# Three layer norms of a two-block transformer: the scaling by the inverse deviation moved from VectorE into the product that turns the tile

## The chip, the cores and the metric

The kernel runs on one core of one Trainium2 chip. The metric is the device time of one execution in microseconds (us). TensorE (PE) has two clocks, 1.2 and 2.4 GHz; the profile gives the granted clock as a share of 2.4 GHz. PEld is TensorE's loading of the stationary operand, DVE is VectorE, ACT is ScalarE, POOL is GpSimd, SP is the engine that issues the weight transfers. ACTq and SPq are the queues through which ACT and SP issue transfers.

## The reference

256 tokens of width 1024 pass through two blocks of two layers each. The change touches the layer norms of the first block alone: the one on the input, the one behind the first mixer and the one behind the feed-forward. Cut to what matters:

```
def layer_norm(x, g, b):
    mu = jnp.mean(xf, axis=-1, keepdims=True)
    xc = xf - mu
    var = jnp.mean(xc * xc, axis=-1, keepdims=True)
    y = xc * lax.rsqrt(var + LN_EPS) * g + b

h = layer_norm(x, ln_in_g, ln_in_b)
for layer in range(DEPTH):                       # DEPTH = 2
    proj = h @ w_in[layer]
    ...
    mix = jnp.concatenate([y_pool, y_sb], axis=-1) @ w_out[layer]
    h = layer_norm(DN_ALPHA * h + mix, ln1_g[layer], ln1_b[layer])
    f = swiglu(h, ...) if layer % 2 == 0 else moe_ffn(h, ...)
    h = layer_norm(DN_ALPHA * h + f, ln2_g[layer], ln2_b[layer])
```

## The kernel before

The 256 tokens are two tiles, t = 0 and 1, of 128 partitions (`TT` = 2). `k.h` holds them with tokens on the partitions. The products need the transpose, features on the partitions, and they are made in float32 from two reduced-precision parts: `k.x[0]` is the high part and `k.x[1]` the rest (low part); a weight is split in the same way into `w_high` (cast by ACT, L358) and `w_low` (DVE, L369). Weights stream from memory in loads of 1 MB, two pieces each, in five raw buffers; `PAIRS` = 4 pieces can stand split ahead of TensorE. A cast of piece n waits until TensorE has used piece n - 4 (`k.used`), and TensorE waits for a piece's low part (`low_made`).

Every engine has its own program, in order; the order is written out by hand and semaphores join the engines. Where a layer norm stands between two runs of products, this happens for each tile:

- DVE adds the residual (`vector_residual`, L628, two instructions), takes the moments (`vector_moments`, L580 to L588), subtracts the mean and multiplies by the gain (`vector_centre`, L594), multiplies by the inverse deviation and adds the shift (`vector_scale`, L604). It signals `normed`.
- ACT makes the inverse deviation in four small steps from the reciprocal of the variance (`scalar_layer_norm`, L614 to L620): a root, a half square, a Newton factor `step`, and `rstd = step * root`, which signals `root`.
- TensorE turns the tile in eight transposes of 128x128 into two banks (`tensor_transposes`, L498), each group of four signalling `turned`. While it waits for a tile it multiplies constants into a bank that nobody reads (`tensor_spin`, L485).
- ACT copies each turned bank to `k.x[0]` (L510, `x_high_made`), DVE subtracts this from the bank for `k.x[1]` (L521, `x_made`).
- The first product (`first_product`, L416 and L422) starts with the high part and takes the low part at the end of each piece.

Tile 1's residual must wait for the last of the product before; tile 0's can start earlier, since `tensor_tail` finishes tile 0 first. A float32 product that is not a transpose shows as two MATMUL instructions in the trace; a transpose shows as one.

The gain and the shift are sent to all 128 partitions of `k.gains` by a transfer of 512 KB each (`scalar_gains`, L662 and L663). For the first norm SP issues them behind the input and ahead of the weights (`sync_first`, L2522).

The site at the start is called the start; the one behind the first mixer, whose turned tiles go into the feed-forward, the feed-forward site; the one behind the feed-forward, ahead of the second mixer, the second mixer's site.

## Time and profile before

| | before |
|---|---|
| time, median of 3 runs (range) | 2132.32 us (2129.55 to 2132.45) |
| span of the profiled execution, first to last instruction | 2127.0 us |
| TensorE busy | 2102.8 us, 99% of the span |
| VectorE busy | 1537.3 us, 72% |
| ScalarE busy | 1349.5 us, 63% |
| mean granted TensorE clock | 0.997 of 2.4 GHz |

The span of the profiled execution is its own time between its first and its last instruction; the 5.3 us by which the median is above it lie outside of these or between executions. Busy shares are means over the whole program. What a change at one place is worth must be read from the waits at that place.

### The profile page before, as it was taken

Reading aid. Unit: us, or ns where it says so; the run is one execution under the profiler, and the core shown is the slowest. Engines: PE = TensorE matmul, PEld = TensorE weight load, DVE = VectorE, ACT = ScalarE, POOL = GpSimd, SP = SyncE. Lnnn points to the kernel's source line nnn. Section 1 sums busy time; section 2 is a strip of 40 time slices with the busy share of each in tenths; the row PEclk is TensorE's granted clock in tenths of the full one; section 3 lists DMA queues with packets and bytes.
Section 4 is the critical chain, followed back from the end, with each engine's and each line's share of the span. In section 5 each row is a group of like instructions: output and inputs, shape, how many; then the busy total and the mean of one; then the engine's idle time right before and its main releaser. Section 6 shows DMA issues by size and latency. Waiting matters only on the chain.

```text
span 2127.0 us, 31761 instructions
## 1 busy us (share of the span) xinstructions
PE 2102.8 (99%) x13318; PEld 1889.9 (89%) x13318; DVE 1537.3 (72%) x1701; ACT 1349.5 (63%) x1610; POOL 48.1 (2%) x45
## 2 busy tenths in 40 slices
PE   9999999999999999999999899999999999999998
PEld 8899989888888888888888799998998999998987
DVE  5565565699999899989999777566654686666544
ACT  5554446688878877887878574574553754755543
POOL 0000000100000000000000000000210000000200
PEclk9999999999999999999999999999999999999999
DMA  9366554499999999999999555634655565545652
GB/s 303 119 206 194 197 183 139 146 362 358 341 358 370 332 375 351 367 337 365 358 364 371 195 185 165 197 126 154 208 199 197 178 190 163 175 147 164 199 198 79
DMA packets 301733, 511.43 MB, mean 240 GB/s; under 512 B 10512, under 2 KB 177552, under 8 KB 301584
## 3 DMA queue, kind: packets, MB, share of 16 engines
q1 hardware_dynamic: 296896, 499.68, 68.8%
q10 hardware_dynamic: 4688, 9.65, 1.4%
q8 instruction: 107, 1.75, 0.3%
q14 instruction: 42, 0.34, 0.0%
HBM read 503.53 MB, written 1.05 MB: 237 GB/s over the span
## 4 chain that ended last, share of the span: by engine, by line
PE 96%; DVE 2%; ACT 1%; issue 0%; DMA 0%; ACTq 0%; DVEq 0%
PE bank L389 28%; PE bank L391 28%; PE bank L390 28%; PE bank L485 2%; PE bank L1851 1%; PE bank L416 1%; PE bank L1428 1%; PE bank L1307 1%; PE bank L1365 1%; PE bank L498 1%; PE bank L422 1%; PE bank L2114 1%; DVE w_low L369 1%; PE bank L2090 0%; PE bank L2099 0%
## 5 line engine op out<-in xcount | busy, mean ns | idle before, releaser
L369 DVE TENSOR_TENSOR w_low<-raw,w_high 128x1024 fp32r<-128x1024 f32 x938 | 1135.9, 1223 | 413.0 <-ACT w_high L358 398.1
L358 ACT CAST w_high<-raw 128x1024 fp32r<-128x1024 f32 x938 | 979.7, 1052 | 454.3 <-PE bank L391 434.9
L389 PE MATMUL bank<-x,w_high 128*128 128x256 f32 x1712 | 478.5, 279 | 0.0
L390 PE MATMUL bank<-x,w_high 128*128 128x256 f32 x1712 | 474.9, 277 | 0.0
L391 PE MATMUL bank<-x,w_low 128*128 128x256 f32 x1712 | 474.9, 277 | 0.0
L389 PE MATMUL bank<-w_high,x 128*128 128x512 f32 (+1 forms) x976 | 342.2, 351 | 0.0
L391 PE MATMUL bank<-w_high,x 128*128 128x512 f32 (+1 forms) x976 | 337.8, 346 | 0.0
L390 PE MATMUL bank<-w_low,x 128*128 128x512 f32 (+1 forms) x976 | 337.8, 346 | 0.0
L389 PEld LDWEIGHTS bank<-x,w_high 128*128 128x128 f32 x1712 | 322.2, 188 | 0.4
L390 PEld LDWEIGHTS bank<-x,w_high 128*128 128x128 f32 x1712 | 322.4, 188 | 0.2
L391 PEld LDWEIGHTS bank<-x,w_low 128*128 128x128 f32 x1712 | 321.7, 188 | 0.0
L391 PEld LDWEIGHTS bank<-w_high,x 128*128 128x128 f32 x976 | 183.2, 188 | 23.5
L389 PEld LDWEIGHTS bank<-w_high,x 128*128 128x128 f32 x976 | 183.4, 188 | 23.1 <-DVE w_low L369 0.6
L390 PEld LDWEIGHTS bank<-w_low,x 128*128 128x128 f32 x976 | 183.4, 188 | 22.1 <-issue 0.5
L389 PE MATMUL bank<-w_high,moe_hidT_high 128*128 128x512 f32 x352 | 138.6, 394 | 0.0
L391 PE MATMUL bank<-w_high,moe_hidT_low 128*128 128x512 f32 x352 | 137.3, 390 | 0.0
L390 PE MATMUL bank<-w_low,moe_hidT_high 128*128 128x512 f32 x352 | 137.1, 389 | 0.0
L389 PE MATMUL bank<-w_high,mlp_hid_high 128*128 128x512 f32 x256 | 99.8, 390 | 0.0
L390 PE MATMUL bank<-w_low,mlp_hid_high 128*128 128x512 f32 x256 | 99.7, 389 | 0.0
L391 PE MATMUL bank<-w_high,mlp_hid_low 128*128 128x512 f32 x256 | 99.6, 389 | 0.0
L391 PEld LDWEIGHTS bank<-w_high,moe_hidT_low 128*128 128x128 f32 x352 | 66.1, 188 | 14.0
L390 PEld LDWEIGHTS bank<-w_low,moe_hidT_high 128*128 128x128 f32 x352 | 66.2, 188 | 13.2
(343 smaller groups left out, 2557.3 us busy)
## 6 DMA issues: line engine op xcount, KB each, us to landing
raw<-in_moe_wd SPq DMA_DIRECT2D x88, 1024.0 KB, 5.8
raw<-in_w_in SPq DMA_DIRECT2D x84, 1024.0 KB, 5.3
raw<-in_moe_wg SPq DMA_DIRECT2D x80, 1024.0 KB, 6.0
raw<-in_moe_wu SPq DMA_DIRECT2D x80, 1024.0 KB, 6.0
raw<-in_w_up SPq DMA_DIRECT2D x32, 1024.0 KB, 5.5
raw<-in_w_down SPq DMA_DIRECT2D x32, 1024.0 KB, 4.9
raw<-in_w_out SPq DMA_DIRECT2D x16, 1024.0 KB, 4.9
raw<-in_ffn_wg SPq DMA_DIRECT2D x11, 1024.0 KB, 5.3
```

Of the source, the lines that this page charges most:

```text
L358: q.copy(high, raw).then_inc(st.cast, 1)
L369: q.tensor_tensor(low, raw, high.bitcast(F32), ALU.subtract).then_inc(st.low_made, 1)
L389: T.matmul(out, stationary[0], moving[0], start=start, stop=False, skip_group_check=True)
L390: T.matmul(out, stationary[0], moving[1], start=False, stop=False, skip_group_check=True)
L391: return T.matmul(out, stationary[1], moving[0], start=False, stop=stop, skip_group_check=True)
L416: T.matmul(out[:, j, :], w[:, kk, j * P:(j + 1) * P], k.x[0][:, i, :], start=(i == 0 and j == 0 and w is piece[0]), stop=False, skip_group ...
L422: mm = T.matmul(out[:, j, :], piece[0][:, kk, j * P:(j + 1) * P], k.x[1][:, i, :], start=False, stop=(i == KT - 1), skip_group_check=True)
L485: k.nc.tensor.matmul(k.banks[bank][:, 0:2 * P], k.shared[:, 0:P], k.shared[:, 0:2 * P], start=True, stop=True)
L498: mm = T.transpose(k.banks[2 * t + g][:, i * P:(i + 1) * P], src[:, t, (4 * g + i) * P:(4 * g + i + 1) * P], ident)
L1307: mm = T.matmul(bank[:, j * width:(j + 1) * width], m.split[w][:, t, kk * P:(kk + 1) * P], m.pick[:, t, 0:width], start=(t == 0), stop=(t ...
L1365: mm = T.matmul(k.banks[banks[i]], u.pickT[:, t, :], u.y[w][:, half * 512:(half + 1) * 512], start=(n == 0), stop=(n == len(parts) - 1))
L1428: mm = T.transpose(unit_bank(k, j)[:, i * P:(i + 1) * P], m.hid_s[j % 2][:, i * P:(i + 1) * P], ident)
```

## The change

At three of the norms, `vector_scale` no longer stands between the centred tile and the transposes. Instead DVE makes a diagonal matrix of the inverse deviations of the tile's 128 tokens (`vector_diagonal`: the identity times `root` times `step`), and TensorE multiplies the centred tile by it (`tensor_scaled`): stationary is a 128x128 block of `k.h`, moving is the diagonal, and the product is the block transposed and scaled. This is a product in float32 and no transpose. The shift is put into the bank ahead of that, by products over a single row (`tensor_shifts`: stationary 1x128 of the shift, moving 1x128 of ones). At the feed-forward site and the second mixer's the constant products of `tensor_spin` are gone; the shifts stand there. The scaled and shifted `k.h`, which the next residual needs, is made later by `vector_scale_late`, between the low parts of the weights.

```
@@ (new functions; the docstrings are empty in the source)
+def tensor_shifts(k, banks, shift, tiles=range(TT)):
+    for t, g in ((t, g) for t in tiles for g in range(2)):
+        for i in range(4):
+            cols = slice((4 * g + i) * P, (4 * g + i + 1) * P)
+            k.nc.tensor.matmul(k.banks[banks[2 * t + g]][:, i * P:(i + 1) * P], shift[:, cols],
+                               k.shared_const("ones")[0:1, :], start=(i == 0), stop=False, skip_group_check=True)
+
+def tensor_scaled(k, banks, t):
+    T = k.nc.tensor
+    T.wait_ge(k.sem("centred"), 2 * (TT * k.transposed + t + 1))
+    for g in range(2):
+        for i in range(4):
+            mm = T.matmul(k.banks[banks[2 * t + g]][:, i * P:(i + 1) * P],
+                          k.h[:, t, (4 * g + i) * P:(4 * g + i + 1) * P], k.diagonal[:, t, :], start=False, stop=True,
+                          skip_group_check=True)
+        mm.then_inc(k.sem("turned"), 1)
+
+def tensor_norm_transposes(k, banks, gains_ready):
+    k.nc.tensor.wait_ge(*gains_ready)
+    for t in range(TT):
+        tensor_shifts(k, banks, k.gains[0:1, 1, :], (t,))
+        tensor_scaled(k, banks, t)
+
+def vector_norm_ahead(k, t, gains_ready):
+    vector_moments(k, t, k.h[:, t, :])
+    k.nc.vector.wait_ge(*gains_ready)
+    vector_centre(k, t, k.h[:, t, :], k.sem("centred"))
+    vector_diagonal(k, t)
+
+def vector_diagonal(k, t):
+    root, step = root_columns(k, t)[2], root_columns(k, t)[4]
+    k.nc.vector.wait_ge(k.sem("stepped"), k.norm_number[t])
+    k.nc.vector.tensor_scalar(k.diagonal[:, t, :], k.shared_const("ident"), root, step, ALU.mult, ALU.mult).then_inc(
+        k.sem("centred"), 1)
+
+def vector_scale_late(k, t, gain_rows=None):
+    V = k.nc.vector
+    V.wait_ge(k.sem("turned"), 4 * k.transposed + 4)
+    k.inverted += 1
+    V.wait_ge(k.sem("root"), k.inverted)
+    V.wait_ge(k.sem("centred"), 2 * (TT * k.transposed + t + 1))
+    V.scalar_tensor_tensor(out=k.h[:, t, :], in0=k.h[:, t, :], scalar=norm_columns(k, t)[2], in1=k.gains[:, 1, :],
+                           op0=ALU.mult, op1=ALU.add).then_inc(k.sem("normed"), 1)
@@ def tensor_mixer
-    T.wait_ge(k.sem("loaded_shared"), 16)
-    tensor_transposes(k, k.h, [[norm_ready(k, t)] for t in range(TT)], 3, (4, 11, 2) if layer else (12, 8, 3))
+    if layer:
+        tensor_norm_transposes(k, range(4), (k.sem("loaded_gains"), 32 * 2))
+    else:
+        T.wait_ge(k.sem("loaded_shared"), 16)
+        T.wait_ge(k.sem("loaded_start"), 32)
+        for half in range(2):
+            mm = T.matmul(k.banks[4 + half], k.shared_const("ones")[0:1, :],
+                          k.first_rows[0][:, half * 512:(half + 1) * 512], start=True, stop=True)
+        mm.then_inc(k.sem("gain_spread"), 1)
+        tensor_shifts(k, range(4), k.first_rows[1])
+        tensor_spin(k, 7, 8)
+        for t in range(TT):
+            tensor_scaled(k, range(4), t)
@@ def tensor_ffn
-    tensor_transposes(k, k.h, [[norm_ready(k, t)] for t in range(TT)], 7, (4, 11, 2))
+    tensor_norm_transposes(k, FFN_TURNS, (k.sem("loaded_gains"), 32))
@@ def vector_mixer, in the loop over pieces p
+        if p in (2, 3):
+            if layer == 0 and p == 2:
+                k.nc.vector.wait_ge(k.sem("loaded_start"), 48)
+            vector_scale_late(k, p - 2)
@@ def vector_ffn, in the loop over j
         vector_lows(k, k.weights, at + PAIRS + 2)
+        if 1 <= j <= TT:
+            vector_scale_late(k, j - 1)
@@ def sync_first
-    for i, name in enumerate(("ln_in_g", "ln_in_b")):
-        q.dma_start(k.gains[:, i, :], k.A[name].partition_broadcast(P)).then_inc(k.sem("loaded_start"), 16)
@@ def scalar_first
+    for row, name in zip(k.first_rows, ("ln_in_g", "ln_in_b")):
+        q.dma_start(row, k.A[name]).then_inc(k.sem("loaded_start"), 16)
     for t in range(TT):
         scalar_layer_norm(k, t)
     scalar_casts(k, k.weights, 0)
-    scalar_transposes(k, (0,))
+    scalar_transposes(k)
     scalar_casts(k, k.weights, 1)
+    q.dma_start(k.gains[:, 1, :], k.A["ln_in_b"].partition_broadcast(P)).then_inc(k.sem("loaded_start"), 16)
     q.dma_start(const, k.A["const_first"]).then_inc(k.sem("loaded_consts"), 16)
     ...
-    scalar_transposes(k, (1,))
     scalar_casts(k, k.weights, PAIRS - 1)
@@ def vector_first
-    V.wait_ge(k.sem("loaded_start"), 32)
+    V.wait_ge(k.sem("gain_spread"), 1)
+    V.wait_ge(k.sem("loaded_shared"), 16)
     for t in range(TT):
-        vector_centre(k, t, k.h[:, t, :])
-        vector_scale(k, t)
+        vector_centre(k, t, k.h[:, t, :], k.sem("centred"), k.psum[:, 4 * 512:6 * 512])
+        vector_diagonal(k, t)
```

Two further moves are in the diff: the transfers of the next norm's gain and shift (`scalar_gains`) are issued some pieces later, behind `vector_scale_late`, and some semaphores share a name (`bounds_made`, `router_parts`).

The next rows are TensorE's at the feed-forward site before the change, from the last products of the mixer to the first of the feed-forward. L485 are the constant products, L498 the transposes.

```order
514 L390 MATMUL bank<-w_low,mixer_mix_high 128x512
515 L391 MATMUL bank<-w_high,mixer_mix_low 128x512
516 L485 MATMUL bank<-shared 128x256 x4
517 L498 MATMUL bank<-shared,h 128x128 [waits normed]
518 L498 MATMUL bank<-shared,h 128x128 x7
519 L485 MATMUL bank<-shared 128x256 x11
520 L498 MATMUL bank<-shared,h 128x128 [waits normed]
521 L498 MATMUL bank<-shared,h 128x128 x7
522 L485 MATMUL bank<-shared 128x256 x2
523 L416 MATMUL bank<-x,w_high 128x256 [waits x_high_made,x_made,low_made]
```

The same place on TensorE after the change; `gains` is the row of the shift, and `norm` is the diagonal, which lies in the memory of `norm1`.

```order
514 L393 MATMUL bank<-w_low,mixer_mix_high 128x512
515 L394 MATMUL bank<-w_high,mixer_mix_low 128x512
516 L512 MATMUL bank<-shared,gains 128x128 [waits loaded_gains]
517 L512 MATMUL bank<-shared,gains 128x128 x7
518 L522 MATMUL bank<-norm,h 128x128 [waits centred]
519 L522 MATMUL bank<-norm,h 128x128 x7
520 L512 MATMUL bank<-shared,gains 128x128 x8
521 L522 MATMUL bank<-norm,h 128x128 [waits centred]
522 L522 MATMUL bank<-norm,h 128x128 x7
523 L419 MATMUL bank<-x,w_high 128x256 [waits x_high_made,x_made,low_made]
```

Seventeen constant products have made place for sixteen shifts, the sixteen transposes for sixteen products with the diagonal, and what these wait for is `centred` in place of `normed`.

The next rows are DVE's at the feed-forward site after the change, from tile 0's centring on (before, both L610 were the full-width scaling, L604, and neither L621 was there).

```order
57 L655 SCALAR_TENSOR_TENSOR h<-h,stats,gains 128x1024 [waits loaded_gains]
58 L610 TENSOR_SCALAR norm<-shared,stats 128x128 [waits stepped]
59 L691 SCALAR_TENSOR_TENSOR h<-h,bank 128x512 [waits used]
...
66 L655 SCALAR_TENSOR_TENSOR h<-h,stats,gains 128x1024 [waits loaded_gains]
67 L610 TENSOR_SCALAR norm<-shared,stats 128x128 [waits stepped]
68 L553 TENSOR_TENSOR x<-bank,x 128x4x128 [waits x_high_made] x4
69 L372 TENSOR_TENSOR w_low<-raw,w_high 128x1024 [waits cast] x6
70 L1127 TENSOR_TENSOR ffn_gate<-bank,ffn_gate 128x512 [waits gate_out,used]
71 L1130 TENSOR_TENSOR ffn_hid_low<-ffn_gate,ffn_hid_high 128x512 [waits hid_high]
72 L372 TENSOR_TENSOR w_low<-raw,w_high 128x1024 [waits cast] x4
73 L621 SCALAR_TENSOR_TENSOR h<-h,stats,gains 128x1024 [waits centred,root,turned]
```

The scaling of both tiles has moved behind the first ten low parts of weights.

The last rows are TensorE's first ones in the program after the change. `second_const` holds the row of the first gain and `gains` the row of the first shift; L488 are constant products.

```order
0 L932 MATMUL bank<-second_const,shared 128x512 [waits barrier_Pool_Activation_PE_DVE_SP_release,loaded_start,loaded_shared]
1 L932 MATMUL bank<-second_const,shared 128x512
2 L512 MATMUL bank<-shared,gains 128x128 x16
3 L488 MATMUL bank<-shared 128x256 x8
4 L522 MATMUL bank<-norm,h 128x128 [waits centred]
5 L522 MATMUL bank<-norm,h 128x128 x7
6 L522 MATMUL bank<-norm,h 128x128 [waits centred]
7 L522 MATMUL bank<-norm,h 128x128 x7
8 L440 MATMUL bank<-x,w_high 128x256 [waits x_high_made,cast]
```

Before, 12 constant products, 8 transposes, 8 constant products, 8 transposes and 3 constant products stood ahead of the first L440 (then L437); now it is 2 wide products that spread the gain over the partitions, 16 shifts, 8 constant products and 16 products with the diagonal.

## Rows read from the trace of the kernel before

**Rows 1.** The page: the span, and the chain that ended last by engine.

```profile
span 2127.0 us, 31761 instructions
PE 96%; DVE 2%; ACT 1%; issue 0%; DMA 0%; ACTq 0%; DVEq 0%
```

**Rows 2.** Timeline of the feed-forward site: start, length, engine, line, operation, count.

```profile
105.59 1.27 DVE L594 SCALAR_TENSOR_TENSOR h<-h,stats,gains 128x1024 f32<-128x1024 f32 x1
106.10 1.71 PEld L485 LDWEIGHTS bank<-shared 128*128 128x128 f32 x8
106.18 0.39 ACT L618 ACTIVATE stats<-stats 128x1 f32<-128x1 f32 x1
107.01 1.28 DVE L604 SCALAR_TENSOR_TENSOR h<-h,stats,gains 128x1024 f32<-128x1024 f32 x1
108.21 1.28 DVE L628 SCALAR_TENSOR_TENSOR h<-h,bank 128x512 f32<-128x512 f32 x2
...
111.35 1.26 DVE L594 SCALAR_TENSOR_TENSOR h<-h,stats,gains 128x1024 f32<-128x1024 f32 x1
112.56 1.05 ACT L510 CAST x<-bank 128x512 fp32r<-128x512 f32 x2
112.77 1.28 DVE L604 SCALAR_TENSOR_TENSOR h<-h,stats,gains 128x1024 f32<-128x1024 f32 x1
114.11 1.09 PE L498 MATMUL bank<-shared,h 128*128 128x128 f32 x8
114.80 0.59 ACT L510 CAST x<-bank 128x512 fp32r<-128x512 f32 x1 [1.19 <-PE bank L498]
...
115.69 0.19 PEld L416 LDWEIGHTS bank<-x,w_high 128*128 128x128 f32 x1
116.63 4.62 DVE L369 TENSOR_TENSOR w_low<-raw,w_high 128x1024 fp32r<-128x1024 f32 x4
```

**Rows 3.** The chain in order of time: the first product's first piece behind it.

```profile
116.07 1.83 PE bank L416 x16
117.89 0.91 PE bank L422 x8
```

**Rows 4.** Timeline of the second mixer's site: the last transposes and the first product.

```profile
303.37 1.09 PE L498 MATMUL bank<-shared,h 128*128 128x128 f32 x8
304.96 0.19 PEld L416 LDWEIGHTS bank<-x,w_high 128*128 128x128 f32 x1
```

**Rows 5.** Timeline inside the first mixer: float32 products 128 wide, two MATMULs each.

```profile
52.51 0.38 PE L734 MATMUL bank<-mixer_soft,first_const 128*128 128x128 f32 x2
52.73 0.39 PE L736 MATMUL bank<-mixer_soft,first_const 128*128 128x128 f32 x2
```

**Rows 6.** Groups by line and form: 64-row product and its load, and DVE 128 wide.

```profile
L726 PE MATMUL bank<-mixer_q,mixer_k 64*128 64x128 f32 x32 | 4.8, 272 | 0.0
L1278 DVE TENSOR_SCALAR moe_pick<-first_const,moe_base,moe_sel 128x128 fp32r<-128x128 f32 x16 | 4.4, 340 | 0.0
```

**Rows 7.** Timeline of the start.

```profile
4.90 7.63 PE L485 MATMUL bank<-shared 128*128 128x256 f32 x24 [4.90 <-DMA shared<-in_const_shared]
9.33 1.28 DVE L594 SCALAR_TENSOR_TENSOR h<-h,stats,gains 128x1024 f32<-128x1024 f32 x1 [0.86 <-DMA gains<-in_ln_in_b]
17.81 0.59 ACT L510 CAST x<-bank 128x512 fp32r<-128x512 f32 x1
18.67 1.29 PE L437 MATMUL bank<-x,w_high 128*128 128x256 f32 x8
```

**Rows 8.** Windows: TensorE's busy time and MATMUL count, granted clock, DMA share, GB/s.

```profile
9.00:10.00 1.00, 1.00 (x6) 1.00 1.09 388
...
1199.00:1200.00 1.00, 1.00 (x3) 0.50 0.00 0
```

**Rows 9.** The chain in order of time: float32 products 512 wide, two MATMULs each.

```profile
1348.12 1.72 PE bank L1843 x4
```

**Rows 10.** The chain in order of time: a stretch without work.

```profile
1189.52 4.85 issue
```

79 lines of the change are left out of this document (50 added, 29 removed).

## The prediction

> **What bounds the kernel now.** I read the page first. The chain that ended last is TensorE for 96% of the span of 2127.0 us [rows 1], so only what makes TensorE's useful work start earlier or later counts, and that is decided at the places where the chain leaves the weight products. Three of these are touched: the start, the feed-forward site and the second mixer's site. There I read the timelines. Behind the last mixer product TensorE loads its first constant product at 106.10; DVE ends centring tile 0 at 106.86, scales it from 107.01 and only then, at 108.21, takes tile 1's residual; tile 1 is centred from 111.35, scaled from 112.77, transposed from 114.11, and the first product begins at 115.69 [rows 2]. The chain of this site is DVE's for both tiles, then the transposes, one copy on ACT, and the constant products that still stand in the queue. The second mixer's site has the same distances: 303.37 to 304.96 is 1.59, 114.11 to 115.69 is 1.58 [rows 2, 4]. At the start TensorE does not wait for DVE at all after its first constants: the last copy of a turned bank begins at 17.81 and the first product at 18.67 [rows 7].
>
> **The feed-forward site, step by step.**
>
> Tile 0 on DVE: the scaling goes. It held DVE from 107.01 to 108.21, 1.20 us, with 0.22 us ahead of it in which DVE had its own centring to wait for (105.59 plus 1.20, as DVE's next start lies 0.07 ahead of an end, is 106.79) [rows 2]. In its place comes the diagonal, one tensor-scalar of 128x128. The nearest row is the pick matrix, also two scalars at 128 columns, 0.34 us; next operations start some 0.07 us before such an end, so 0.27 us of the queue [rows 6]. It needs `step`, which ACT has at 106.57 [rows 2], before DVE is free: no wait. The diagonal costs 0.27, tile 1's residual starts at 107.06 in place of 108.21: 1.15 us earlier. Bounds for the diagonal: 0.15 us (under half the row) and 0.34.
>
> Tile 1 on DVE: centring starts at 111.35 - 1.15 = 110.20 and frees DVE at 111.40; the diagonal ends at 111.74. Before, the transposes began 0.06 us behind DVE's end (112.77 + 1.28 = 114.05, then 114.11) [rows 2]; now the scaled products begin at 111.80.
>
> TensorE ahead of it: a float32 product 128 wide takes 0.22 us (52.51 to 52.73, two MATMULs each) [rows 5], eight take 1.78 against 0.87 for eight transposes. No row has a stationary operand of one row. The nearest has 64 rows and takes 272 ns a MATMUL like the full ones [rows 6], so I take 0.22 for a shift too; if its weight load, 0.19 as for L416 [rows 2], were not hidden, it would be 0.38, eight of them 3.0. So: shifts 106.10 to 107.88, scaled tile 0 to 109.66, shifts to 111.44, 0.36 us idle, scaled tile 1 from 111.80 to 113.58.
>
> From there: tile 1's first group leaves the array 0.89 + 0.16 behind 111.80, at 112.85; ACT copies from 112.94, as it did 0.09 behind the group's end, for 0.59, to 113.53 [rows 2]. Tile 0's copies (112.56 before) sit behind ACT's steps for tile 1 and move 1.15 earlier with them. TensorE is itself free at 113.58. The first product starts at 113.6, in place of 115.69: **2.1 us earlier**. Of this 1.15 is tile 0's scaling, 1.1 is tile 1's (centring to turning took 2.76 us, 111.35 to 114.11, and takes 1.60), 0.3 are the last constant products, less the 0.45 us by which the first group is slower as products (1.15 + 1.1 + 0.3 - 0.45 = 2.1).
>
> What is late next: the first product uses 24 MATMULs of its first piece in 1.83 + 0.91 = 2.74 us [rows 3], so it wants the next piece's low part at 116.34. DVE makes this behind the four low parts of x. Those ended at about 116.63 [rows 2]; now the last copy on ACT ends at 114.4, the low part of x at 115.1, and the weight's at 115.07 + 1.22 = 116.3. The slack was 0.6 us before and is nearly nothing now. I count no loss; each 0.1 us that DVE is later is lost in full.
>
> The second mixer's site has the same program: 2.1 us more. **Both sites: -4.2 us.**
>
> The late scalings are two of 1.28 us on DVE at each site. They stand where DVE has 4.6 us of low parts for four pieces [rows 2] that TensorE uses in 11 us [rows 3]; with four pieces split ahead they are hidden. I put them at nothing; uncovered they would cost 1.28 each, 7.7 in all.
>
> **The start.** SP no longer sends 1 MB of gains, so weights land earlier, which nobody waits for. TensorE begins when the two rows of 4 KB have landed, issued on ACT's queue behind the constants, which landed at 4.90 [rows 7]. I take 5.2, with 4.9 and 7.5 as bounds. Then two products 512 wide. Two such products are four MATMULs, 1.72 us at full clock [rows 9] and 3.45 at half. And the first work goes at half clock: the 24 constant MATMULs took 7.5 us up to the transposes at 12.36 and would take 24 x 0.216 = 5.2 at the pace of a warm site (8 in 1.71) [rows 2, 7]; half speed loses half of its time, so some 4.5 us went at 1.2 GHz, to about 9.4. (The granted clock says 1.00 at 9 [rows 8]; in these first microseconds the pace decides.) So the wide products end at 8.65. DVE can then centre from about 9.0, as before at 9.33, and has both diagonals at 12. But TensorE's own queue is longer: 16 shifts take 3.55 at full clock and 0.35 more for the rest of the half clock, to 12.5; 8 constant products 3.45, to 16.0; 16 scaled products 3.55, to 19.5. ACT has the third bank copied by then. The first product starts at 19.55 in place of 18.67: **+0.9 us**. Behind it stand ACT's cast of piece 1, now behind all four copies (ready at 21.3, wanted at 21.4), and the constants, now issued some 6 us later behind another 512 KB: by the 388 GB/s at the start [rows 8] 1.5 MB needs 4 us, so they land at 27 to 28, and TensorE wants them at 30. Both just pass.
>
> **Sum:** -4.2 + 0.9 = -3.3 us on the span: 2123.7. The median of the runs is 5.3 us above the span; 2132.3 - 3.3 is **2129.0 us**.
>
> **A page against the rows.** The spacing of float32 MATMULs 128 wide with a weight load each is 0.11 us here [rows 5]. The Trainium skill, "TensorE: Matmul & The Clock Gate", section "Back-to-back issue gap", gives some 81 ns for a load and a matmul of N=128 in a stream. By that, eight products would take 1.3 us and not 1.78, each site would gain 0.3 us more (by the first group's copy) and the start 1.9; the sum would be -5.8. The trace's rows do not agree, and the sum goes by them.
>
> **Rivals.**
>
> *The clock stays low at the start.* Products of one row may not bring TensorE to its full clock as full ones do. No row has one; for it speaks only that 4.5 us of work were needed before the pace doubled. Then the wide products end at 8.65, the shifts at 15.75 (7.1), the constant products run 4.5 us at half clock and 1.3 at full, to 21.5, the scaled ones end at 25.1: 6.4 us later than before. Sum +2.2, 2134.5 us.
>
> *Slower: the clock falls at the two sites.* The constant products stood there and are gone. After 4.85 us without work, which ended at 1194.4, the granted clock is 0.50 and still that at 1199 [rows 8, 10]; at these sites it is 1.00 before. If shifts hold the clock no better than idling, it falls during tile 0 and the scaled products and second shifts take 3.55 each: from 107.9 to 111.4, 115.0 and 118.5, which is 2.8 behind 115.69, and three more us at half clock, as work did not bring it back for five us at 1199, cost 1.5. That is +4.3 a site, with the slow start +15.0: 2147.3 us. It decides once the clock falls before about 110 in a site. Against it: TensorE's longest idle stretch in a site shrinks to 0.4 us. The Trainium skill (same page, "Part 1: The HAM clock gate") has the array at half rate when it has been idle, which by itself speaks for neither here.
>
> *The low parts are late.* If the diagonal or the copies are slower, the second piece is waited for: up to 0.6 us a site, sum -2.1: 2130.2 us.
>
> *Shifts are slow.* At 3.0 a tile the scaled products of tile 1 begin 2.1 later: the sites give nothing and the start is 2.4 worse. I include this with the others.
>
> *Products are fast,* at 0.16 us for one and not 0.22: two sites of 0.3 and the start's 1.9 more, -5.8, 2126.5 us.
>
> **Chances.** Forecast 0.52; clock low at the start 0.15; clock falls at the sites 0.08; low parts late 0.10; fast products 0.05; the rest, slow shifts or a late row or constants, 0.10. The forecast's own spread is about 1.3 us each way, and 0.2% is 4.3 us, about what a measurement of this kernel can tell from no change. So a quarter of the forecast's chance lies beyond it (0.13), with the fast products and some of the rest 0.22 for faster; slower is the falling clock and some of the rest, 0.13; within 0.2% 0.65. The range 2125.5 to 2135.0 leaves out the falling clock and the ends; the forecast's own is 2127.7 to 2130.3.
>
> **What the profile will show.** Right: at the feed-forward site a diagonal of about 0.3 us, tile 1's scaled products 3.9 us behind the start of tile 0's, the first product 2.1 us earlier against the last mixer product, clock 1.00, less than 0.5 us of idle TensorE, and no wait for `w_low` behind the first piece; at the start the first product at 19 to 20. Wrong: MATMULs of the shifts above 0.15 us apart; a granted clock under 1.00 at the sites; a pace of 0.2 us for the shifts at the start; a stall of TensorE at 27 to 35 us, when the constants or DVE's wait for the shift are late.

## The result, and the profile after

The changed kernel takes 2141.49 us (median of 6 runs, 2137.74 to 2145.95), the kernel before, run beside it, 2131.58 us (6 runs, 2128.80 to 2132.45). The ratio is 1.0049, with a 95% interval of 1.0040 to 1.0059: half a per cent slower, where 2129.0 us was forecast. The profiled execution took 2137.74 us with a span of 2136.4 us, which is 9.4 us more than the span of before [rows 1]. The page of the changed kernel, its first row and the chain that ended last by engine:

```profile
span 2136.4 us, 31870 instructions
PE 96%; DVE 2%; ACT 1%; issue 0%; DMA 0%; ACTq 0%; DVEq 0%
```

TensorE is still the chain, so the 9.4 us must be found at the three places. The chain in order of time, at the start of the changed kernel:

```profile
1.75 4.43 DMA gains<-in_ln_in_b
...
6.31 3.75 PE bank L932 x4
10.06 6.83 PE bank L512 x32
16.88 6.44 PE bank L488 x16
23.32 3.57 PE bank L522 x32
26.89 5.76 PE bank L440 x48
```

L932 are the two wide products that spread the gain (four MATMULs), L512 the shifts, L488 the constant products, L522 the scaled products, L440 the first product of the first mixer. The first product now starts in the timeline at 26.77, against 18.67 [rows 7]: +8.1 us. Four wide MATMULs took 3.75 us, against 1.72 at full clock [rows 9]. The 32 shift MATMULs took 6.83, 0.213 us each, against 0.11 for full float32 products of the same width [rows 5]. Only inside the constant products does the pace rise: 16 of them take 6.44 us, 0.40 each, where a warm site has eight in 1.71 [rows 2]. The 32 scaled MATMULs then take 0.112 each. The first 10.6 us of work, all of it with one row of the stationary and one of the moving operand, went at half the full pace, that of 1.2 GHz. The trace's own list of clock changes agrees: its first entry is the rise to full clock, at 22.49 us in the changed kernel and at 9.34 in the kernel before.

The feed-forward site, timeline of the changed kernel. L394 is the last mixer product, L655 DVE's centring, L610 the diagonal, L691 tile 1's residual, L522 tile 1's scaled products, L419 the first product of the feed-forward layer:

```profile
114.07 0.39 PE L394 MATMUL bank<-w_high,mixer_mix_low 128*128 128x512 f32 x1
...
115.02 1.27 DVE L691 SCALAR_TENSOR_TENSOR h<-h,bank 128x512 f32<-128x512 f32 x2
...
118.16 1.27 DVE L655 SCALAR_TENSOR_TENSOR h<-h,stats,gains 128x1024 f32<-128x1024 f32 x1
...
119.34 0.34 DVE L610 TENSOR_SCALAR norm<-shared,stats 128x128 f32<-128x128 f32 x1
...
120.33 2.77 PE L522 MATMUL bank<-norm,h 128*128 128x128 f32 x16
...
122.75 0.56 PE L419 MATMUL bank<-x,w_high 128*128 128x256 f32 x1
```

The same two places in the timeline of the kernel before, which need one more row each than the front shows, the last product ahead of either site:

```profile
106.09 0.39 PE L391 MATMUL bank<-w_high,mixer_mix_low 128*128 128x512 f32 x1
...
295.36 0.39 PE L391 MATMUL bank<-w_high,ffn_hid_low 128*128 128x512 f32 x1
```

From the last mixer product's start, tile 1's residual begins after 0.95 us (115.02 less 114.07; before 108.21 less 106.09 = 2.12, [rows 2]) and tile 1's centring after 4.09 (5.26 before). DVE is earlier by 1.17 us, where 1.15 was forecast. But the first product comes 8.68 us behind the last mixer product (122.75 less 114.07). It was 9.63 before (its weight load started at 115.69 [rows 2], its MATMUL 0.03 later), so 0.95 us were won and not 2.1. The chain in order of time shows where the rest went, and that more is lost behind it. Changed kernel, feed-forward site:

```profile
114.46 1.98 PE bank L512 x16
116.44 1.98 PE bank L522 x16
...
120.40 2.70 PE bank L522 x16
123.09 2.73 PE bank L419 x16
```

The first part was lost at full clock. Tile 1's scaled products begin 6.26 us behind the last mixer product's start (120.33 less 114.07), although its diagonal was ready at 119.68: TensorE's own queue was late. Sixteen MATMULs take 1.98 us here, one-row and scaled ones alike. Inside such a group the starts lie 0.111 us apart, as between full products, but each change from one-row to full products or back costs some 0.2 us. The second part is the clock's. The last scaled products take 2.70 us and the first piece's first 16 MATMULs 2.73, against 1.83 [rows 3]. The windows of the changed kernel over that place (us, TensorE's busy time and count, then PEld, DVE, ACT, POOL, and the granted clock, DMA share and GB/s):

```profile
120.00:121.40 1.40, 1.40 (x13) 1.28 (x12) 1.26 (x2) 0.42 (x1) 0.00 (x0) 1.00 0.00 0
121.50:123.00 1.50, 1.50 (x9) 1.50 (x9) 0.69 (x1) 0.59 (x1) 0.00 (x0) 0.50 0.00 0
...
125.00:127.00 2.00, 2.00 (x20) 2.00 (x19) 2.00 (x3) 0.17 (x1) 0.00 (x0) 1.00 0.94 359
```

TensorE is busy for all of each window, and all the same the granted clock goes from 1.00 to 0.50 at about 121.5, inside tile 1's scaled products, and is back at 125. The second mixer's site has the same, twice. Its rows in the chain of the changed kernel:

```profile
305.67 3.56 PE bank L522 x16
...
311.22 2.39 PE bank L522 x16
313.61 3.03 PE bank L419 x16
```

There tile 0's scaled products go at half clock as well (3.56 against 1.98), and the first product's start is 9.95 us behind the last product of the layer before (303.31 to 313.26 in the timeline), where it was 9.62 behind it. The sum over the three places: +8.1 at the start; -0.95 + 0.9 at the feed-forward site; +0.33 + 1.2 at the second mixer's. That is +9.6 us, against 9.4 in the spans. Nothing further on differs by more than it does between two executions of one kernel (below).

### The profile page after: what moved, and what is told of

It reads as the page before. It is cut to its first block, busy times and chain, and to the rows that moved or that the text cites. A ratio compares the mean times of both kernels' runs of the same rounds, so it can differ in the third digit from the quotient of the medians.

```text
span 2136.4 us, 31870 instructions
## 1 busy us (share of the span) xinstructions
PE 2109.9 (99%) x13368; PEld 1897.5 (89%) x13368; DVE 1539.3 (72%) x1707; ACT 1350.2 (63%) x1610; POOL 48.5 (2%) x45
## 4 chain that ended last, share of the span: by engine, by line
PE 96%; DVE 2%; ACT 1%; issue 0%; DMA 0%; ACTq 0%; DVEq 0%
PE bank L392 28%; PE bank L394 28%; PE bank L393 28%; PE bank L1948 1%; PE bank L419 1%; PE bank L1525 1%; PE bank L488 1%; PE bank L1404 1%; PE bank L512 1%; PE bank L522 1%; PE bank L1462 1%; PE bank L425 1%; PE bank L2211 1%; DVE w_low L372 1%; PE bank L2187 0%; PE bank L2196 0%
## 5 line engine op out<-in xcount | busy, mean ns | idle before, releaser
L394 PE MATMUL bank<-x,w_low 128*128 128x256 f32 x1712 | 475.3, 278 | 0.0
L394 PE MATMUL bank<-w_high,x 128*128 128x512 f32 (+1 forms) x976 | 338.1, 346 | 0.0
L394 PEld LDWEIGHTS bank<-x,w_low 128*128 128x128 f32 x1712 | 321.9, 188 | 0.0
L394 PEld LDWEIGHTS bank<-w_high,x 128*128 128x128 f32 x976 | 183.4, 188 | 23.6
L392 PEld LDWEIGHTS bank<-w_high,x 128*128 128x128 f32 x976 | 183.6, 188 | 22.9 <-DVE w_low L372 0.6
L394 PE MATMUL bank<-w_high,moe_hidT_low 128*128 128x512 f32 x352 | 137.4, 390 | 0.0
L394 PE MATMUL bank<-w_high,mlp_hid_low 128*128 128x512 f32 x256 | 99.7, 390 | 0.0
L394 PEld LDWEIGHTS bank<-w_high,moe_hidT_low 128*128 128x128 f32 x352 | 66.1, 188 | 13.9
```

The costliest lines, as they stand in the source:

```text
L392: T.matmul(out, stationary[0], moving[0], start=start, stop=False, skip_group_check=True)
L394: return T.matmul(out, stationary[1], moving[0], start=False, stop=stop, skip_group_check=True)
```

## The experiments

Two theories stood against each other. *One row:* products whose operands have one row neither bring TensorE to 2.4 GHz nor keep it there. *Queue:* the places lose for another reason: the order of the products, the landing of the rows, the constant products that are missing at the sites, or products that are only 128 wide. All ratios are to runs of the kernel before on the same chip in the same batch. The three batches ran on three chips, and the medians of the kernel before were 2130.11 us for the first four (26 runs), 2128.55 for the next four (23) and 2132.36 for the last four (9).

### Each half of the change alone

Only the sites (the start is that of the kernel before):

```diff
-        T.wait_ge(k.sem("loaded_start"), 32)
-        for half in range(2):
-            mm = T.matmul(k.banks[4 + half], k.shared_const("ones")[0:1, :],
...
-        tensor_shifts(k, range(4), k.first_rows[1])
-        tensor_spin(k, 7, 8)
-        for t in range(TT):
-            tensor_scaled(k, range(4), t)
+        tensor_transposes(k, k.h, [[norm_ready(k, t)] for t in range(TT)], 3, (12, 8, 3))
```

> The start is that of the kernel before (gains sent by SP, scaling on DVE, 12, 8 and 3 constant products, transposes); only the feed-forward site and the second mixer's are changed. By the two traces, the start lost 7.9 us of the 9.4, the feed-forward site nothing and the second mixer's site 1.5. Theory 1 (one-row products do not hold TensorE's clock, the cost falls in all three places): 0 to 4 us slower than before, about 2133, with stretches of granted clock 0.50 at 115 to 125 and 295 to 310. Rival (the clock at the sites falls only because the start shifted the program, or by chance): -4 us, 2127.5, clock 1.00 at both sites.

Measured: 2132.21 us (10 runs), ratio 1.0004 (0.9990 to 1.0017). In the profiled execution the feed-forward site takes 12.19 us from the last mixer product to the first product, against 9.62, and the second site 8.18. Windows of this kernel in the first site, columns as above:

```profile
110.00:115.00 5.00, 5.00 (x24) 4.78 (x23) 3.28 (x8) 2.17 (x7) 0.00 (x0) 0.50 0.01 3
115.00:120.00 5.00, 5.00 (x24) 4.78 (x24) 1.02 (x2) 1.17 (x2) 0.00 (x0) 0.50 0.00 0
```

The clock fell here too, with an old start; where it falls differs from one execution to the next and from site to site. At the second site of this execution it stayed at 1.00. The timeline there:

```profile
303.16 2.05 PE L512 MATMUL bank<-shared,gains 1*128 1x128 f32 x16
305.14 2.05 PE L522 MATMUL bank<-norm,h 128*128 128x128 f32 x16
307.06 0.36 PE L419 MATMUL bank<-x,w_high 128*128 128x256 f32 x1
```

The 8.18 us of this site are what one-row shifts give when the clock holds. The sites together win nothing that can be measured.

Only the start (the sites are those of the kernel before):

```diff
-    tensor_norm_transposes(k, FFN_TURNS, (k.sem("loaded_gains"), 32))
+    tensor_transposes(k, k.h, [[norm_ready(k, t)] for t in range(TT)], 7, (4, 11, 2))
...
-    vector_residual_norm_ahead(k, SUMS, base + N_FFN, (k.sem("loaded_gains"), 32 * 2))
+    vector_residual_norm(k, SUMS, base + N_FFN, (k.sem("loaded_gains"), 32 * 2))
```

> The changed start alone, the two sites are those of the kernel before. Theory 1: all of the start's loss is here, 8 us slower than before (2139 to 2140), the first product near 26.8. Rival (the loss of the changed kernel sits in the sites or comes with the late scalings and gains transfers): within 2 us of before.

Measured: 2141.41 us (5 runs), ratio 1.0040 (1.0019 to 1.0061). The timeline has the shifts at half pace again and the first product at 26.37, 7.7 us later than before; both sites are back at 9.63. So the start carries most of the loss.

### The shift as a product over all 128 rows

The gains lie in SBUF on every partition. The same sum in the bank can therefore be made by a full product: the shift's 128 columns from all partitions as the stationary operand and the identity as the moving one. It puts the shift of one column into every element of its row, as the one-row product does. The changed kernel with this at the two sites; its start stays as changed:

```diff
-            k.nc.tensor.matmul(k.banks[banks[2 * t + g]][:, i * P:(i + 1) * P], shift[:, cols],
-                               k.shared_const("ones")[0:1, :], start=(i == 0), stop=False, skip_group_check=True)
+            moving = k.shared_const("ident" if shift.shape[0] == P else "ones")[0:shift.shape[0], :]
+            k.nc.tensor.matmul(k.banks[banks[2 * t + g]][:, i * P:(i + 1) * P], shift[:, cols], moving,
+                               start=(i == 0), stop=False, skip_group_check=True)
...
-        tensor_shifts(k, banks, k.gains[0:1, 1, :], (t,))
+        tensor_shifts(k, banks, k.gains[:, 1, :], (t,))
```

> The changed kernel with the shifts of the two sites made by products over 128 rows: stationary is a 128x128 block of the shift as it already lies in all partitions, moving is the identity; same results, same count, same width. Only the rows differ. Theory 1 (one-row products do not hold the clock): granted clock 1.00 at both sites, first products 2.1 us a site earlier against the last product before than in the kernel before, so 5.6 us faster than the changed kernel, about 2136. Rival (the narrow products of 128 columns, or the missing constant products, let the clock fall, whatever the rows): the clock falls as before and the time stays at 2141.

Measured: 2137.12 us (10 runs), ratio 1.0029 (1.0014 to 1.0045). The feed-forward site in the timeline of this kernel (L513 are the shifts, L523 the scaled products of tile 1):

```profile
114.18 0.39 PE L394 MATMUL bank<-w_high,mixer_mix_low 128*128 128x512 f32 x1
114.41 1.95 PE L513 MATMUL bank<-shared,gains 128*128 128x128 f32 x16
...
119.84 2.05 PE L523 MATMUL bank<-norm,h 128*128 128x128 f32 x16
...
121.77 0.36 PE L419 MATMUL bank<-x,w_high 128*128 128x256 f32 x1
```

and its windows over both sites (TensorE alone):

```profile
114.00:118.00 4.00, 4.00 (x36) 1.00 0.02 4
...
305.00:309.00 4.00, 4.00 (x36) 1.00 0.25 66
```

121.77 less 114.18 is 7.59 us, at both sites, against 9.62: -2.03 each, where the forecast had -2.1. The clock is 1.00 throughout. The products stand in the same order, are as narrow, and no constant product stands between them. What changed are the rows of the shift, and with them the moving values, the identity in place of ones. Of the gain over the changed kernel some 0.6 us a site (8.18 less 7.59) come without the clock: no change between one-row and full products is left.

With the old start and these sites (the edits of the first and the third kernel together):

> The start of the kernel before and both sites changed with shifts over 128 rows. Theory 1: 4.2 us faster than before, about 2127.4, clock 1.00 at both sites. Rival (narrow products let the clock fall): 0 to 4 us slower than before, as sites alone.

Measured: 2129.05 us (10 runs), ratio 0.9997 (0.9982 to 1.0012). The trace is as expected at all three places (first product 19.2, sites 7.58 and 7.59, span 2121.7, 5.3 less than before), but the timed median does not show the 4 us. The interval reaches to 0.9982, and 4 us are 0.9981. This was the first sign that executions of one kernel differ by something that the touched places don't explain.

### What raises the clock at the start

The eight constant products, put ahead of the one-row products:

```diff
         T.wait_ge(k.sem("loaded_shared"), 16)
+        tensor_spin(k, 7, 8)
         T.wait_ge(k.sem("loaded_start"), 32)
...
         tensor_shifts(k, range(4), k.first_rows[1])
-        tensor_spin(k, 7, 8)
```

> The changed kernel, but at the start the 8 constant products stand ahead of the one-row products and not behind them. Theory 1 (one-row products neither raise nor hold the clock): the constant products run from 4.9, the clock rises during or just after them (9 to 11 us), the wide products and shifts then run at 0.43 and 0.12 us a MATMUL and the clock falls again while or after the shifts run, so the products with the diagonal go at half clock in part; the first product at 20 to 23, against 26.8. Rival (any work raises and holds the clock, it only rose late for another reason): no second fall, the first product at 20.

Measured: 2139.77 us (one execution). The timeline of its start on TensorE, lines as above, but one off for L933:

```profile
10.73 1.98 PE L933 MATMUL bank<-second_const,shared 1*128 1x512 f32 x4
12.55 3.94 PE L512 MATMUL bank<-shared,gains 1*128 1x128 f32 x32
16.42 5.21 PE L522 MATMUL bank<-norm,h 128*128 128x128 f32 x32
21.51 1.15 PE L440 MATMUL bank<-x,w_high 128*128 128x256 f32 x8
```

and its windows:

```profile
12.00:15.90 3.90, 3.90 (x33) 3.53 (x32) 3.15 (x5) 0.00 (x0) 0.00 (x0) 1.00 1.10 348
16.00:19.20 3.20, 3.20 (x16) 2.98 (x15) 0.92 (x2) 0.58 (x1) 0.00 (x0) 0.50 1.10 348
```

The clock's first entry, its rise, is at 9.10 us, inside the constant products. Behind these the wide products take 1.98 us in place of 3.75, and the shifts 3.94 in place of 7.03. But after 5 us of one-row products the clock falls, at 15.92, although TensorE has not paused, and the scaled products pay for it (16 MATMULs in 3.2 us). The first product is at 21.51, 5.3 us better than the changed kernel and 2.8 worse than before. The whole time is nearly that of the changed kernel all the same, because in this execution both sites had half clock too, for 10.2 us from 111.5 and for 3.4 from 312.9, and the feed-forward layer ran at its slower pace (below).

No constant products at all at the changed start:

```diff
         tensor_shifts(k, range(4), k.first_rows[1])
-        tensor_spin(k, 7, 8)
         for t in range(TT):
             tensor_scaled(k, range(4), t)
```

> The changed kernel with the 8 constant products of the start left out. Theory 1: shifts end at 16.9 at half clock and the products with the diagonal, full ones, begin at half clock too; the clock rises only 3.5 us or more behind their beginning, at 20.5 or later; first product at 22.5 to 24. Rival (any work raises the clock after long enough): the clock rises between 13 and 18, in or just behind the one-row products, and the first product comes at 20.5 to 21.

Measured: 2133.08 us (one execution), first product at 23.25. Its scaled products in the timeline:

```profile
17.16 6.22 PE L522 MATMUL bank<-norm,h 128*128 128x128 f32 x32
```

With nothing but one-row products ahead of them, the full scaled products begin at half pace and take 6.22 us in place of 3.73. The rise is entered at 22.19 us, 5.0 us behind the first scaled product. 10.5 us of one-row work had brought nothing; the clock rose behind full products, scaled ones here and constant ones in the other kernels.

The start with no one-row product: gains and shift are broadcast by SP's queue as in the kernel before, four constant products stand ahead, the shifts go over 128 rows. The diagonal and scaled products stay.

```diff
         T.wait_ge(k.sem("loaded_shared"), 16)
+        tensor_spin(k, 7, 4)
         T.wait_ge(k.sem("loaded_start"), 32)
-        for half in range(2):
-            mm = T.matmul(k.banks[4 + half], k.shared_const("ones")[0:1, :],
...
-        tensor_shifts(k, range(4), k.first_rows[1])
-        tensor_spin(k, 7, 8)
+        tensor_shifts(k, range(4), k.gains[:, 1, :])
```

> No one-row product is left: at the start the gains come as before by SP to all partitions, 4 constant products, then 16 shifts over 128 rows with the identity, then the products with the diagonal, none behind; the sites as in the run with full-row shifts. Theory 1: the clock rises at 9 to 11 and stays; first product at 16.5 to 17.5; with 4.5 us from the sites 6 us faster than before, about 2125. Rival (narrow products of 128 columns do not raise the clock either): the clock rises after 12 and the first product comes at 19 or later.

Measured: 2129.00 us (12 runs), ratio 0.9996 (0.9987 to 1.0006). Its timeline:

```profile
9.46 3.84 PE L513 MATMUL bank<-shared,gains 128*128 128x128 f32 x32 [0.85 <-DMA gains<-in_ln_in_b]
13.14 3.74 PE L523 MATMUL bank<-norm,h 128*128 128x128 f32 x32
16.75 1.18 PE L440 MATMUL bank<-x,w_high 128*128 128x256 f32 x8
```

The clock rose at 8.14, inside the four constant products, so this start doesn't tell whether the narrow products would have raised it. The shifts go at full pace (3.84 for 32) and the first product starts at 16.75, 1.9 us earlier than before and 10.0 earlier than in the changed kernel, with sites of 7.59 and 7.60. The places together win 6 us on the trace (1.9 and twice 2.0). The ratio of 0.9996 is 0.9 us, and its interval reaches to 0.9987, which is 2.8 us. So a part of what the places give was lost elsewhere in the executions that were timed. The last section has the one candidate that the traces show.

The kernel before with fewer constant products at its start, as a control of what they cost there:

```diff
-    tensor_transposes(k, k.h, [[norm_ready(k, t)] for t in range(TT)], 3, (4, 11, 2) if layer else (12, 8, 3))
+    tensor_transposes(k, k.h, [[norm_ready(k, t)] for t in range(TT)], 3, (4, 11, 2) if layer else (12, 3, 0))
```

> The kernel before with 12, 3 and 0 constant products at its start in place of 12, 8 and 3, nothing else. If these only stand in the way (tile 1 is normed at 14.45, its transposes began at 16.5), the first product comes at 15.8 to 16.5 in place of 18.7 and the kernel is 2 to 3 us faster than before; if the clock needs them, the first products run at half clock and nothing is gained.

Measured: 2128.78 us (11 runs), ratio 0.9998 (0.9989 to 1.0007); first product at 16.27, 2.4 us earlier than 18.67 [rows 7]. Eight of the constant products at the old start are not needed for the clock, which is 1.00 behind them all the same; they only stand in the queue. The timed median doesn't show the gain: the interval reaches to 0.9989, which is 2.3 us. The profiled execution gave the 2.4 us back at the norm of the experts' layer near 1190, which took 2.5 us more.

### The direct test: one-row constant products in the kernel before

Nothing of the change is in this kernel. At the two sites, the constant products of the kernel before use one row of the same operands and not 128; their number, place and width stay. Their result is read by nobody.

```diff
 def tensor_spin(k, bank, times):
-
+    rows = slice(0, 1) if k.transposed in (1, 2) else slice(0, P)
     for _ in range(times):
-        k.nc.tensor.matmul(k.banks[bank][:, 0:2 * P], k.shared[:, 0:P], k.shared[:, 0:2 * P], start=True, stop=True)
+        k.nc.tensor.matmul(k.banks[bank][:, 0:2 * P], k.shared[rows, 0:P], k.shared[rows, 0:2 * P], start=True, stop=True)
```

> The kernel before with one edit: the constant products at the feed-forward site and the second mixer's (4, 11 and 2 at each) use one row in place of 128; count, width, transposes, scaling on DVE stay. Theory 1 (one-row products do not hold TensorE's clock): granted clock 0.50 in both sites, from some microseconds after the one-row products begin, and the first products at half clock for a while; 1 to 4 us a site, 2 to 7 us slower than before. Rival (the diagonal's products, not the rows, let it fall): clock 1.00 in both sites, same time as before.

Measured: 2149.57 us (4 runs), ratio 1.0082 (1.0064 to 1.0100). Its timeline at the feed-forward site and its windows:

```profile
105.95 1.99 PE L485 MATMUL bank<-shared 1*128 1x256 f32 x8
...
108.91 7.94 PE L485 MATMUL bank<-shared 1*128 1x256 f32 x22
...
120.68 0.58 PE L416 MATMUL bank<-x,w_high 128*128 128x256 f32 x1
```

```profile
106.00:110.00 4.00, 4.00 (x22) 3.17 (x22) 3.81 (x6) 3.23 (x5) 0.00 (x0) 1.00 0.00 0
111.00:115.00 4.00, 4.00 (x11) 3.06 (x11) 3.64 (x4) 2.05 (x6) 0.00 (x0) 0.50 0.00 0
...
313.00:317.00 4.00, 4.00 (x11) 2.97 (x9) 2.63 (x4) 1.25 (x3) 0.00 (x0) 0.50 0.23 66
```

Between 106 and 110 there are 22 MATMULs in 4 us at full clock (eight of them the narrower transposes), between 111 and 115 11 at half, and TensorE is busy in every microsecond of both. The sites take 15.05 and 14.66 us in place of 9.62, some 10.5 us together. Half clock goes on behind them to 124.5 and 325.8 us; half of these 3.8 and 4.6 us, by an estimate, is lost, 4.2 in all. That makes 14.7 of the 17.2 us between the medians. The profiled execution has a span of 2149.9 us, 22.9 more than before: its feed-forward layer also ran at the slower pace of the last section, and later stages took longer too. Only the number of rows of the constant products differs from the kernel before, so *one row* is shown as what takes the clock away, and *queue* keeps no more than the 0.6 us a site above. No run separates the row of the stationary operand from that of the moving one or from the values in them, and no count between one and 128 was tried. The Trainium skill, "TensorE: Matmul & The Clock Gate", "Part 1: The HAM clock gate", tells of a gate that follows how busy the array has lately been; by the profile's busy time this trace does not agree, since a TensorE busy for 4.00 of 4.00 us is at half clock. The same page, "Why this matters for your kernels", has a single matmul of 32 rows take the time of a full one. No run here has 32 rows; at full clock one-row MATMULs 256 wide start 0.216 us apart in this trace and full ones 0.216 in that of before, so for one row the trace agrees, apart from the 0.2 us at each change.

### The version that the experiments point to, and two repeats

Old start with 12, 3 and 0 constant products, both sites with the diagonal and shifts over 128 rows (the sites of the fourth kernel, the start of the kernel with fewer constant products):

> The start of the kernel before with 12, 3 and 0 constant products, and both sites with the diagonal and full-row shifts. The start gives 2.4 us by the trace of the run with fewer constant products, the sites 2.0 and 0.1 each by the runs with full-row shifts: 6.6 us faster than before if all stages keep their pace, 0.3%. Rival (what the sites and the start gain is given back in the stages behind them, by a slower pace of the weight products): within 2 us of before, with a pace of 117 to 118 ns in one of the stages.

Measured: 2124.64 us (5 runs, 2121.53 to 2127.16), ratio 0.9963 (0.9949 to 0.9976), the only kernel here whose timed median is clearly below that of the kernel before. The first product in its timeline:

```profile
16.24 1.18 PE L440 MATMUL bank<-x,w_high 128*128 128x256 f32 x8 [0.33 <-ACT x L543]
```

First product at 16.24 (-2.4), sites 7.58 and 7.59 (-4.1): 6.5 us by the trace, 7.9 us by the ratio, whose interval (5.1 to 10.9) holds it.

The full-row start and the kernel before were each run and profiled once more, without an edit, to see what differs between executions:

> The kernel without any one-row product once more, unchanged, to look at one more execution. In its first one the weight products of the feed-forward stood 117.8 ns apart all through the stage, against 113.3 in seven other kernels' executions, which cost 4.7 us. If this pace is drawn anew in each execution: 113.3 or 117.8 in this stage or another, and a time that follows it. If it belongs to the kernel: 117.8 again in this stage.

> The kernel before once more, unchanged. Its runs reach from 2126.9 to 2136.2 us. If the pace of the weight products is drawn anew in each execution, the stages show 113.3 or 117.8 ns in another pattern than in its first profile, and the difference of the two spans is the sum of the stages' differences.

Measured: 2124.98 us and 2130.17 us. What they show stands in the last section.

## Why the prediction was wrong

**The step that failed** is one sentence of the working at the site, "No row has a stationary operand of one row. The nearest has 64 rows and takes 272 ns a MATMUL like the full ones, so I take 0.22 for a shift too", with its use at the start, where one-row products were counted as the work that ends the half clock. For the shift itself at full clock the price held: 0.111 us from one MATMUL to the next. The sum put the change between one-row and full products at nothing, and it cost some 0.2 us each time, 0.6 us a site (8.18 at full clock against 7.59). As work for the clock the step was wrong, and that is the larger part. A row on 64 rows says nothing of one row, and nothing in the trace of before did; the estimate of 4.5 us at 1.2 GHz was taken from full products and carried over.

**The start** was put at +0.9 and measured +8.1. The terms: the rows landed at 6.31 and not 5.2, inside the bound (+1.1); the wide products took 3.54 us, as forecast (3.45); the shifts took 6.96 (9.85 to 16.81) and not 3.85 (+3.1); the constant products 6.35 and not 3.5 (+2.9); the scaled products 3.6, as forecast. This is the rival "the clock stays low at the start", which got 0.15 and +6.4; the remainder is the later row, and 6.35 for the constant products against 5.8.

**The two sites** were put at -2.1 each. Measured against before: 0 at the first (-0.95 to the first product, +0.9 in it) and +1.5 at the second (+0.33 and +1.2). That the first came out at 0 is a gain and a loss that happen to cancel. Of what was lost against the forecast, 0.6 us a site is the changes between one-row and full products, and the clock's half pace is the rest: 1.4 us at the first site (0.5 ahead of the first product and 0.9 in it) and 3.0 at the second (1.8 and 1.2). DVE's steps were right in each part: diagonal 0.34, tile 1's residual 1.15 us earlier, its centring 4.09 behind the last mixer product (4.11 forecast). With shifts over 128 rows the whole is right: -2.03 at either site. (The forecast let TensorE's queue begin with the weight load at 106.10, where a MATMUL begins 0.22 us later; the 0.36 us of idle time in its sum had room for that.) What failed is that the clock was taken as given; this is the rival "the clock falls at the two sites" (0.08), at a smaller price than its 4.3 us a site. It was said to decide only if the clock fell before about 110. That point lies 3.9 us behind the last mixer product. In the changed kernel it fell 7.4 us behind it at the first site, at 121.5, but only 2.5 us behind the last product at the second, at 305.8, and there tile 0's scaled products paid 1.6 us; in the kernel with the sites alone it fell at 109.9, 3.4 us behind, and the first product came 2.6 us later than before (12.19 against 9.62).

**"Against it: TensorE's longest idle stretch in a site shrinks to 0.4 us"** was the argument that kept that rival small. The stretch shrank (no idle row stands between L512 and L522), and the clock fell regardless. A stretch without idle time was no evidence for the clock here, where one-row products fill a part of it.

**Steps that held:** the late scalings are hidden (six of 1.28 us on DVE; the feed-forward layer takes 179.55 us with full-row shifts, from its first product to its last, and 179.64 before); the second piece's low part came in time (with full-row shifts, the first piece's 16 and 8 MATMULs took 1.94 and 0.91 us, against 1.83 and 0.91 [rows 3], with no gap behind them); the constants at the start were not waited for (48 MATMULs of L440 in 5.76 us without a gap, and the first mixer took 87.3 us from its first product to its last, 87.4 before). The pace of 81 ns that the prediction gives from the Trainium skill, "TensorE: Matmul & The Clock Gate", "Back-to-back issue gap", showed nowhere: full-row float32 MATMULs 128 wide take 0.111 us in a stream (1.78 for 16).

**The sum:** +8.1, 0 and +1.5 us against +0.9, -2.1 and -2.1: 12.9 us too fast, of which 7.2 at the start and 5.7 at the sites. The measured 2141.49 lies beyond the upper end of the range, 2135.0. One unknown, what one-row products do to the clock, stood under all three terms. The two rivals that came true have that one cause. The prediction joined them only in the sum of the second, 2147.3 us, to which it gave 0.08, and the range left this one out.

## What to carry to other kernels

Before one-row products take the place of full ones on a TensorE-bound path, look at what the granted clock does behind them, not only at their own duration: here they cost nothing in themselves (0.111 us a MATMUL either way), 0.2 us at each change between the two kinds, and up to 6 us a place through the clock (the start's shifts and constant products against the forecast). If a vector has to be added in a bank and lies broadcast in SBUF, a product over all rows with the identity does it at the price of a full product and keeps the clock. Constant products are worth counting too: those that only stand in the queue ahead of ready data cost their time (2.4 us at this start, in the timeline).

## What the runs showed of the hardware that was not expected

**One-row products and the clock** (above): neither raised (10.6 us of them at the start) nor held (in the kernel before, with them in place of full constant products, half clock from 110.8 for 13.7 us and from 312.2 for 13.7 us), with TensorE busy all the time. A few of them between full products do not always let it fall. Four kernels have one-row shifts at both sites; in their profiled executions the clock fell inside the site six times of eight. Five executions have full-row shifts there, and it fell in none of their ten sites.

**At the start the windows' granted clock doesn't tell the pace.** In the changed kernel it reads 1.00 between 10 and 12 us, with 12 MATMULs counted in 2 us, where the sites with full-row shifts have 36 in 4, and with 0.213 us from one to the next in the chain. The trace has no entry of the clock before its first rise, at 22.49 us, and the windows show 1.00 where there is none. The count beside the clock tells the pace there.

**A whole stage of weight products runs at one of two paces, drawn anew in each execution.** The same kernel, the one with the full-row start, in its two profiled executions, timeline of TensorE inside the feed-forward layer. First execution:

```profile
199.82 0.28 PE L393 MATMUL bank<-x,w_high 128*128 128x256 f32 x1
...
201.24 0.28 PE L393 MATMUL bank<-x,w_high 128*128 128x256 f32 x1
```

Second execution:

```profile
199.76 0.28 PE L392 MATMUL bank<-x,w_high 128*128 128x256 f32 x1
...
201.12 0.28 PE L392 MATMUL bank<-x,w_high 128*128 128x256 f32 x1
```

Between the two rows stand eleven more MATMULs in either, twelve steps: 1.42 us in the first, 118 ns a step, and 1.36 in the second, 113 ns. The granted clock is 1.00 in both. Over the stage, from its first product to that of the next layer, it is 191.9 against 187.2 us, 4.7 us. In the second execution it was another stage, the feed-forward part between 1481 and 1666, that went slowly (184.1 us against 180.6), and the kernel before shows the same there between its two executions. No edit of this study touches the later stage. In the feed-forward layer the edits move only the late scalings, and the kernel with one-row constant products, which has none of them, ran slowly there too. It fits the spread of the kernel before, 2126.88 to 2136.16 us over 26 runs, and it may be why an edit of 4 us could be read at the places and not in a median of ten runs. What sets the pace stays open, and so does whether a kernel's start changes the odds: the full-row start's 6 us on the trace against its 0.9996 (0.9987 to 1.0006) is not fully explained by it, since the kernel with the trimmed old start, with nearly the same gain at the places, showed all of it. The two were timed on different chips. The second execution of the full-row start, on the chip of the trimmed one, took 2124.98 us against a median of 2132.36 for the kernel before there, about as much less as the trimmed one, so the chip or the batch is the likelier difference; one execution doesn't show it.
